# Channel sums of the mixer's bands: one fp32 matmul with ones, or two fp32r matmuls of split halves

## What is computed

```python
def step(S, inp):
    qc, kc, vc, gc = inp
    G = jnp.cumsum(gc, axis=2)
    o = jnp.einsum('nhtk,nhkv->nhtv', qc * jnp.exp(G), S)
    decay = jnp.exp(jnp.where(causal, G[:, :, :, None] - G[:, :, None], NEG))
    A = jnp.einsum('nhtk,nhsk,nhtsk->nhts', qc, kc, decay)
    o = o + jnp.einsum('nhts,nhsv->nhtv', A, vc)
```

## Time and profile before

| | us |
|---|---|
| median of 3 runs (lowest, highest) | 2831.27 (2830.68, 2840.25) |
| span of the profiled execution | 2832.5 |
| PE busy | 2714.8 (96%) |
| DVE busy | 1729.9 (61%) |
| POOL busy | 1244.1 (44%) |
| ACT busy | 1111.1 (39%) |

### The profile page before, as it was taken

The page is one execution under the profiler, slowest core; times in us unless marked ns, Lnnn a source line. Parts: engine busy times, 40 slices in busy tenths (PEclk is TensorE's granted clock), DMA queues, the critical chain, the costliest instruction groups (busy, mean ns, idle before and its releaser), DMA issues.

```text
span 2832.5 us, 63047 instructions
## 1 busy us (share of the span) xinstructions
PE 2714.8 (96%) x22569; PEld 2513.5 (89%) x22569; DVE 1729.9 (61%) x3199; ACT 1111.1 (39%) x2499; POOL 1244.1 (44%) x1296
## 2 busy tenths in 40 slices
PE   6999999998999999999989999999998999999999
PEld 5898999998999999999877787878788999999998
DVE  4777678665333346896466566666676343447984
ACT  5121212354444445442543233332364444444444
POOL 4000000455555566454754333333376666665544
PEclk8999999999999999999999999999999999999999
DMA  7422111545777755743233424243453444457443
GB/s 255 142 76 91 53 39 38 196 134 153 202 204 211 216 163 165 249 157 96 62 119 102 151 90 150 92 120 125 141 185 93 127 133 128 135 168 251 158 140 112
DMA packets 385193, 398.00 MB, mean 141 GB/s; under 512 B 27587, under 2 KB 346678, under 8 KB 383046
## 3 DMA queue, kind: packets, MB, share of 16 engines
q1 hardware_dynamic: 362994, 363.57, 41.2%
q10 hardware_dynamic: 13780, 23.05, 2.3%
q0 software_dynamic: 8192, 8.40, 1.1%
HBM read 291.46 MB, written 103.48 MB: 139 GB/s over the span
## 4 chain that ended last, share of the span: by engine, by line
PE 77%; DVE 10%; issue 4%; DMA 3%; ACT 3%; POOL 2%; SPq 1%; DVEq 0%; POOLq 0%; ACTq 0%
PE bank L4030 19%; PE bank L4031 18%; PE bank L4032 18%; PE bank L4654 2%; PE bank L4773 2%; PE bank L4675 2%; DVE stage L3487 1%; PE bank L4159 1%; POOL op_l L1397 1%; PE bank L4696 1%; DVE xT L3516 1%; DVE td L3493 1%; PE bank L4321 1%; DVE xT L3509 1%; PE bank L4293 1%
## 5 line engine op out<-in xcount | busy, mean ns | idle before, releaser
L1397 POOL TENSOR_TENSOR op_l<-raw,op_h 128x512 fp32r<-128x512 f32 (+1 forms) x396 | 522.7, 1325 | 416.3 <-ACT op_h L2066 402.3
L4030 PE MATMUL bank<-t_high,op_h 128*128 128x258 f32 x1736 | 497.9, 287 | 14.9 <-ACT tq L2094 8.0
L4031 PE MATMUL bank<-t_low,op_h 128*128 128x258 f32 x1736 | 493.5, 284 | 0.0
L4032 PE MATMUL bank<-t_high,op_l 128*128 128x258 f32 x1736 | 491.0, 283 | 0.0
L4030 PE MATMUL bank<-hh,whi 128*128 128x344 f32 (+3 forms) x1324 | 439.9, 332 | 29.0 <-POOL wlo L1257 8.1
L4032 PE MATMUL bank<-hh,wlo 128*128 128x344 f32 (+3 forms) x1324 | 423.0, 320 | 0.0
L4031 PE MATMUL bank<-hl,whi 128*128 128x344 f32 (+3 forms) x1324 | 423.0, 319 | 0.0
L4030 PEld LDWEIGHTS bank<-t_high,op_h 128*128 128x128 f32 x1736 | 329.3, 190 | 28.6 <-issue 23.8
L4031 PEld LDWEIGHTS bank<-t_low,op_h 128*128 128x128 f32 x1736 | 331.2, 191 | 0.0
L4032 PEld LDWEIGHTS bank<-t_high,op_l 128*128 128x128 f32 x1736 | 330.6, 190 | 0.0
L4030 PE MATMUL bank<-td,op_h 128*128 128x258 f32 x1008 | 288.8, 286 | 21.6 <-DVE xT L3516 20.3
(11 more groups left out here) (521 smaller groups left out, 6278.4 us busy)
## 6 DMA issues: line engine op xcount, KB each, us to landing
raw<-in_w_gu SPq DMA_DIRECT2D x84, 512.0 KB, 4.8
pk<-in_cache_ckv SPq DMA_DIRECT2D x256, 128.0 KB, 2.4
ada_x<-in_w_ada SPq DMA_DIRECT2D x28, 1024.0 KB, 8.7
act_high<-st_all SPq DMA_DIRECT2D x86, 258.0 KB, 5.7
act_low<-st_all SPq DMA_DIRECT2D x86, 258.0 KB, 5.7
act_raw<-tq SPq DMA_DIRECT2D x164, 129.0 KB, 4.0
raw<-in_w_down SPq DMA_DIRECT2D x48, 384.0 KB, 4.5
wst<-in_w_in_even SPq DMA_DIRECT2D x28, 512.0 KB
```

Source lines behind the costliest of these rows:

```text
L1397: nc.gpsimd.tensor_tensor(op_l[p][:, 0:t.half, :], op_source(p, t), op_h[p][:, 0:t.half, :].bitcast(F), ALU.subtract).then_inc(op_lo.sem, 1)
L4030: mm(out, wh_, xh_, start=start, stop=False, skip_group_check=more)
L4031: mm(out, wh_, xl_, start=False, stop=False, skip_group_check=more)
L4032: return mm(out, wl_, xh_, start=False, stop=stop, skip_group_check=more)
```

## The change

The channel sum of a piece becomes two fp32r matmuls into the same bank: of its high half, which ScalarE rounds (`band_high`), and of its low half, which DVE subtracts (`band_low`). The halves lie in rows h and h + 4 of x (two buffers each), so ScalarE waits in head 0 for x to be saved. `ones_r` is a rounded tile of ones, made by GpSimd. DVE's order changes: lows of pieces 0 and 1 stand ahead of `chunk_products`; product(j + 2) now stands ahead of the wait for the sum of j, and band_low(j + 2) behind weigh(j). The low halves of the weights of slots s + 3 to s + 6 go from DVE to GpSimd (`mixer` there); those of s + 2, s + 7 and s + 8 stay with DVE. ScalarE's band_high are put between its copies. The first semaphores are shared with later users by counts.

```diff
+        band = [[nc.alloc_sbuf_tensor_at(f"band{e}{h}", [P, 2, 512], R, offset=w_at - 3 * KT * N * 4 + (h + e * HEADS) * N * 4)
+                 for e in range(2)] for h in range(HEADS)]
...
@@ gpsimd
+            def mixer():
+                for h in range(HEADS):
+                    for u in range(3, 7):
+                        if h == 0 and u == 4:
+                            pool.wait_ge(ada_part, CG * ADA_MIX)
+                            nc.gpsimd.tensor_copy(ones_r[:], ones[:]).then_inc(band_hi, 1)
+                        g = G_IN + 7 * h + u
+                        pool.wait_ge(w_hi, g + 1)
+                        pool.wait_ge(w_split, g + 2)
+                        nc.gpsimd.tensor_tensor(wlo[g % 2][:], wst[g % 2][:], whi[g % 2][:].bitcast(F), ALU.subtract).then_inc(w_split, 1)
...
@@ scalar, in the head
+                    def band_high(j):
+                        d, _, nb = PIECES[j]
+                        w = nb * (BL - d)
+                        act.wait_ge(e_ready, NBAND * h + j + 1)
+                        if j > 1:
+                            act.wait_ge(bc_ready[j % 2], BC[j % 2] * h + j // 2)
+                        nc.scalar.copy(band[h][0][:, j % 2, 0:w], ed[j % 2][:, 0:w]).then_inc(band_hi, 1)
...
+                    if h == 0:
+                        act.wait_ge(x_saved, 16)
+                        act.wait_ge(band_hi, 1)
+                    band_high(0)
+                    band_high(1)
                     split_high(s + 4)
                     for c in range(NC):
                         filled(SLOT_CG, c)
                         nc.scalar.copy(ug[:, 2 + c * CW:2 + (c + 1) * CW], bank[c][:, 0:CW]).then_inc(bank_free[c], 1)
                         if c < 2:
                             tokens(c, vtok[:, 4 * c:4 * c + 4, :])
+                        band_high(2 * c + 2)
+                        band_high(2 * c + 3)
                     split_high(s + 5)
+                    for j in range(8, NBAND):
+                        band_high(j)
                     split_high(s + 6)
...
@@ vector, in the head
             def split_low(g):
                 dve.wait_ge(w_hi, g + 1)
+                dve.wait_ge(w_split, g + 2)
...
+                def band_low(n):
+                    d, _, nb = PIECES[n]
+                    w = nb * (BL - d)
+                    dve.wait_ge(band_hi, NBAND * h + n + 1 + 1)
+                    v.tensor_tensor(band[h][1][:, n % 2, 0:w], ed[n % 2][:, 0:w], band[h][0][:, n % 2, 0:w].bitcast(F), ALU.subtract
+                                    ).then_inc(band_lo, 1)
+                    dve.wait_ge(band_lo, NBAND * h + n + 1)
...
-                split_low(s + 3)
                 product(0)
                 product(1)
+                band_low(0)
+                band_low(1)
                 chunk_products()
...
                 for n in range(0, 12, 2):
                     for j in (n, n + 1):
+                        if j + 2 < NBAND:
+                            product(j + 2)
                         dve.wait_ge(bc_ready[j % 2], BC[j % 2] * h + j // 2 + 1)
-                        if j + 2 < 12:
-                            product(j + 2)
                         weigh(j)
+                        if j + 2 < NBAND:
+                            band_low(j + 2)
                     keys(n // 2 + 3)
                     if n >= 6:
                         conv_input((n - 6) // 2)
-                    if n == 0:
-                        split_low(s + 4)
-                    elif n == 4:
-                        split_low(s + 5)
-                split_low(s + 6)
...
@@ tensor
                     pe.wait_ge(bc_free[n % 2], BC[n % 2] * h + n // 2 + 1)
-                    pe.wait_ge(e_ready, 12 * h + n + 1)
-                    mm(bank[6 + n % 2][:, 0:w], ones[:], ed[n % 2][:, 0:w], start=True, stop=True).then_inc(bc_ready[n % 2], 1)
+                    pe.wait_ge(band_lo, NBAND * h + n + 1)
+                    mm(bank[6 + n % 2][:, 0:w], ones_r[:], band[h][0][:, n % 2, 0:w], start=True, stop=False)
+                    mm(bank[6 + n % 2][:, 0:w], ones_r[:], band[h][1][:, n % 2, 0:w], start=False, stop=True).then_inc(bc_ready[n % 2], 1)
```

More of the change, by code:

```diff
@@ L81 @@
 PIECES = [(d, h * NBL // 2, NBL // 2) for d in range(4) for h in range(2)] + [(d, 0, NBL) for d in range(4, BL)]
+NBAND = len(PIECES)
 AW = 256
@@ L457, in trunk @@
         s0 = lay("mix", "s0", [P, NS, P])
+        ones_r = lay("mix", "ones_r", [P, P], R)
         most = 6
@@ L733, in trunk @@
             sem, ("fill_ready", "fill_out", "q_ready", "ds_ready", "dn_ready", "dp_ready", "pv_ready", "da_ready", "dw_ready", "lm_ready"))
-        os_ready, os_taken, own_part, own_taken, xs_bank, xs_ready = map(
-            sem, ("os_ready", "os_taken", "own_part", "own_taken", "xs_bank", "xs_ready"))
+        band_hi, band_lo, own_part, own_taken, xs_bank, xs_ready = map(
+            sem, ("band_hi", "band_lo", "own_part", "own_taken", "xs_bank", "xs_ready"))
+        os_ready, os_taken = Count(band_hi, NBAND * HEADS + 1), Count(band_lo, NBAND * HEADS)
         masks_ready, newmask_ready, knew_ready, sw_used = map(
@@ L1614, in _ @@
             pool.sem_inc(acc_ready, NC * (KT - 1))
-            phases = [setup, out_proj, lambda: gated(0, G_FFN0, 2), latents, pairs,
+            phases = [setup, mixer, out_proj, lambda: gated(0, G_FFN0, 2), latents, pairs,
                       lambda: gated(1, G_DOWN1, 6), lambda: None]
@@ L3907, in sample_outputs @@
             def sample_outputs():
-                dve.wait_ge(os_ready, 1)
-                v.tensor_copy(os32[:], bank[4][:, 0:MH * NS].rearrange("p (h n) -> p h n", h=MH)).then_inc(os_taken, 1)
+                dve.wait_ge(*os_ready(1))
+                v.tensor_copy(os32[:], bank[4][:, 0:MH * NS].rearrange("p (h n) -> p h n", h=MH)).then_inc(os_taken.sem, 1)
             def own_rows():
@@ L4840, in sample_values @@
                                  start=ct == 0, stop=ct == CT - 1)
-                ins.then_inc(os_ready, 1)
+                ins.then_inc(os_ready.sem, 1)
             def sample_outputs():
-                pe.wait_ge(os_taken, 1)
+                pe.wait_ge(*os_taken(1))
                 pe.wait_ge(wow_loaded, 64)
```

## The result

The changed kernel takes 2843.1 us, the median of 7 runs (2840.81 to 2847.71); in the same rounds the kernel before took 2831.27 us (2828.14 to 2840.25). The ratio is 1.0033, with a 95% interval of 1.0020 to 1.0046. So the change makes the kernel slower by 9 us (the ratio) to 12 us (the two medians); I had forecast 2.8 us faster, and 2843.1 lies beyond the upper end of my range, 2838. The loss is under the 0.5% that I had taken for what a measurement can tell from no change, but the interval lies clear of 1.

What follows compares the result with a forecast made beforehand. PE was taken to bound the mixer: 13.5 us spared by fp32r sums, minus 10.9 us of waiting for late DVE, gives 2.6 us gained, 2831.3 to 2828.7, say 2828.5 us; range 2817 to 2838.

Steps and rivals of the forecast that it cites:

- What bounds the kernel: Even layer's mixer: PE, busy 447.83 of 450 us, sets the time; other engines cost nothing until PE meets their semaphores.
- Term 1: Band sums on PE: two fp32r matmuls replace one fp32 matmul, sparing PE 3.37 us a head, 13.5 in all.
- Rival D: New band matmuls bound by weight loads: PE gains only 6.0 us, time 2826 to 2831; chance 0.08.
- Term 3: GpSimd's weight subtractions slow DVE by 1.2 us (slot s + 5) and 0.3 (slot s + 4) a head.
- Term 2: DVE's work up to keys(7): DVE 1.8 us late in heads 0, 2 and 3, so PE waits; no stall in head 1.
- the round trip: DVE's hand-over to ScalarE and back on band 2: 0.3 us once a head, later hidden behind two-part weighs.
- the wait for band 2: DVE still waits 0.65 us for band 2, because PE has a projection part in between.
- The pauses: PE stands still for late DVE before attend(7): 3.3 us each in heads 0, 2, 3 and 1.0 in head 1.
- rival C: DVE collapses: round trips of 0.5 us in ten bands, GpSimd subtractions biting at 1.6 us; 2838 to 2851 us; chance 0.14.
- the clock was taken as 1.00 for good: PE's granted clock read as 1.00 in the mixer's stage from 95 to 545 us; no fall was charged.
- Edits at nothing: ScalarE's band_high, ones_r, the wait for saved x, weight loads and DVE's wait for band_high 0 and 1 cost nothing.
- The tightest one: Head 0's modulation, delayed by DVE's wait for band_high 0 and 1, still reaches PE with 0.6 us to spare.

Runs made afterwards that it cites:

- reorder8: Changed kernel with eight of twelve bands split, weights' low halves all on DVE, chunk_products and slot s + 4's low half moved earlier: 2819.24 us, 0.9955 of before.
- warm: Changed kernel plus spare PE matmuls ahead of its waits for keys(5) and keys(7), results overwritten: 2837.81 us, ratio 1.0013 to the kernel before.
- late5: Kernel before plus six unused DVE additions of 512 columns ahead of keys(5): 2847.75 us, ratio 1.0054 to the kernel before.
- first6: Changed kernel with only bands 0 to 5 split, the other six summed in fp32, weights' low halves all on DVE: 2822.48 us, 0.9962 of before.
- pool6: first6 with the weights' low halves of slots s+3 to s+6 on GpSimd: 2831.55 us, ratio 0.9996 to the kernel before.
- pool_only: Kernel before with only the weights' low halves of slots s+3 to s+6 moved to GpSimd, sums still fp32: 2833.96 us, ratio 1.0001.
- reorder6: first6 with chunk_products ahead of band_low(0) and slot s + 4's low half ahead of the loop in heads 1 to 3: 2823.94 us, 0.9966 of before.

## Why the prediction was wrong

**What bounds the kernel** ("a microsecond off PE's queue is a microsecond off the kernel") was right while PE had no pauses: reorder8 was spared 9.6 us and its mixer ended 10.1 earlier.

**Term 1, right, and a little small.** PE's timeline in head 2, the pair of bands 0 and 1, before and then after:

```profile
342.74 0.60 PE L4312 MATMUL bank<-ident,hv 128*128 128x128 f32 x4
343.18 1.88 PE L4321 MATMUL bank<-ed,ones 128*128 128x512 f32 x4
344.99 1.10 PE L4293 MATMUL bank<-qb,ki 128*64 128x8 f32 x32
```

```profile
350.49 0.60 PE L4356 MATMUL bank<-ident,hv 128*128 128x128 f32 x4
350.85 0.48 PE L4365 MATMUL bank<-band,ones_r 128*128 128x512 f32 x1
351.17 0.39 PE L4366 MATMUL bank<-band,ones_r 128*128 128x512 f32 x1
...
351.62 0.40 PE L4366 MATMUL bank<-band,ones_r 128*128 128x512 f32 x1
```

From the start of the transposes to attend(2), at 351.95, it is 1.46 us, against 2.25 before: 0.79 saved, 0.71 forecast. The pair of 448 columns saves 0.70, forecast 0.6. By their starts, where PE works at full clock, the six pairs save 0.79, 0.70, 0.60, 0.49, 0.70 and 0.25, which is 3.5 us a head and 14.1 in all, for 3.37 and 13.5. Rival D is out.

**The step that failed: Term 3, the price of GpSimd beside DVE.** I charged DVE 0.3 us for the subtraction of slot s + 4 and 1.2 for that of slot s + 5, 1.5 us a head, from a range of 0 to 1.6. Each cost 2.1, 4.2 us a head: 3.71 us for the chunk products that take 1.57 before, 2.80 for a keys operation of 0.7. I misread as a slowdown between two values. Both rows there follow one rule: the DVE operation that starts second waits for GpSimd's to end (604.91 + 2.86 = 607.77, 604.30 + 2.38 = 606.68, and then its own 1.1), the one that starts first, at 544.54, isn't held. So the subtraction that cost DVE 1.23 us in its own list costs it 2.1 on GpSimd, and the move makes DVE later by 0.9 us each, not earlier.

What that did to the sum can be read from attend(1) to attend(7). PE is spared 3.5 us in each of these stretches, and still they last 2.0, -0.1, 1.7 and 1.6 us longer than before. So DVE is late by 5.5, 3.5, 5.2 and 5.2 us, 19.3 in all (0.3 of it, in head 1, is the clock's), where I had 3.3, 1.0, 3.3 and 3.3, 10.9 in all. The 2.7 us a head by which Term 3 is too small cover the difference; two charges of Term 2 that didn't come, the round trip and the wait for band 2, take some back. With this the loops are not 2.6 us shorter but 5.2 longer.

**The pauses looked right by luck.** I expected 10.9 us of pauses, and PE's idle time rose by 12.3, of which the waits for keys are 9.2; head 2 pauses 2.35 + 0.55 us at keys(5) and keys(7) and 0.2 before, 3.1 for 3.3. That isn't the lateness of DVE, 5.2 us there: PE spent another part of it at half clock instead of standing still, and was spared a little more than I had said. The larger pause also stands at keys(5), two steps ahead of where I looked. The transfer of the wait from DVE to PE took place as told.

**Term 2, the round trip.** I gave it 0.3 us; on DVE's and ScalarE's timelines of head 2, band 2's high half starts at 354.04 and DVE's low half at 354.71, 0.1 us behind the weigh that covers it. The 0.65 us of waiting for band 2 didn't come either, since DVE, held at the chunk products, began to weigh band 0 only at 353.92, 2.4 us after its matmuls had ended (351.17 + 0.39). So one half of rival C is out (0.5 us of round trip in each of ten bands); its other half, GpSimd's subtractions biting harder than I had charged, is what came.

**The second step that failed: the clock was taken as 1.00 for good.** The earlier trace rows has it at 1.00, and I charged a pause its own length only. In the changed kernel the clock fell to its lower level behind six of the eight pauses of over 0.4 us in the loops, all but the 1.6 us one in head 0 and the 0.50 us one in head 3. This added little to the time: four stretches stand where DVE sets the pace and cost 0.3 us together, as warm and the two profiles of head 0 show, and the two behind attend(7) cost 3.1. Late5 shows that pauses alone bring the fall about in the old kernel, and that it costs 1.5 us a stretch where nothing else waits. How long the clock stays down, and which pause it falls behind, I can't derive.

**The rest, open.** 13.6 us more at half clock at the samples' outputs add some 6.2 us, and a wait for DVE in head 3 (L4383) 0.9. Together, against before: 5.2 in the loops, 3.1 behind attend(7), 6.2 at the outputs and 0.9, less 0.3 by which head 0 begins earlier, are 15.1 us, measured 15.2. Kernels without any pause have stretches at the outputs too, first6 17.0 us, and reorder8 has only the 3.4 of the kernel before. So this part goes neither with the pauses nor plainly with the new sums, and I know no cause for it.

**Edits at nothing** held in the main. No wait for ones_r or for weights shows in PE's list. DVE waits for ScalarE only at band_high(0), 5.2 and 4.7 us in heads 0 and 1 and 1.4 in heads 2 and 3, where it waited for PE before. The tightest one didn't hold: PE's wait of 1.6 us for DVE's queue (L4356, head 0) is the modulation's hand-over, of which I said "0.6 to spare". DVE comes to it late because the chunk products ahead of it take 3.70 instead of 1.57 us beside GpSimd, the same 2.1 us.

## What to carry to other kernels

Where one engine is the bound and has no pauses, a saving on it counts only as far as the engines that feed it keep their margin: work out the margin first, and convert only as much as it covers (eight bands of twelve gained 0.45%, twelve gained nothing measurable even without GpSimd). A pause of TensorE can bring its clock down behind it, and a busy column won't show that: in late5 9.6 us of pauses took 1.5 us more in each of three of four cases. But before you charge it, ask which engine sets TensorE's next wait. Where the late engine sets that one too, the slower clock only shortens the next pause (40.35 us with it, 40.38 without). So judge how late an engine is by the distance between two points where it is waited for, not by the idle time of the engine that waits. And before work goes from VectorE to an idle GpSimd, charge VectorE the full length of GpSimd's instruction whenever VectorE's next operations have both inputs in SBUF: here 2.1 us paid for 1.23 spared.

## What the runs showed of the hardware that I had not expected

- Behind most pauses of 1.4 to 2.65 us TensorE's granted clock fell to its lower level 0.7 to 2.3 us after work had begun again, and behind two of the changed kernel's three pauses of some 0.5 us at keys(7) too. The length of the pause alone doesn't decide: the clock stayed up behind the 1.6 us in head 0 (in both profiles of the changed kernel, in warm and in pool6), behind one of late5's of 2.65 us, and behind 1.46 us in one of two profiles of the same kernel. Behind the 0.42 us of pool_only and the 0.65 us of pool6 it stayed up as well.
- Time at the lower level costs nothing where TensorE would have waited for VectorE anyway: attend(5) to attend(7) in head 0 took 13.39 us at a mean clock of 0.87 and 13.36 at 1.00.
- At the lower level matmuls of 344 columns start 0.29 us apart instead of 0.157, while PE is shown 100% busy.
- A VectorE operation with two SBUF inputs that starts just behind a GpSimd subtraction of 128x1024 ends with it or later: 2.1 us more, for a 128x128 operation as for a 128x512 one.
- The half clock at the samples' outputs comes and goes from kernel to kernel (3.4 us before, 17.0 in first6, 13.6 in reorder6, 3.4 in reorder8), and spare matmuls among the one-column ones left it. Its cause is open.
